# Eight-head decayed scores: two 64-row matmuls per head pair merged into one 128-row matmul against a zero-padded query operand

## The reference

```python
def step(state, xs):                       # one chunk of 64 tokens, all heads
    qc, kc, gc, vc = xs
    cum = jnp.cumsum(gc, axis=2)           # running sum of log f
    diff = cum[:, :, :, None, :] - cum[:, :, None, :, :]
    decay = jnp.exp(jnp.where(causal[:, :, None], diff, -jnp.inf))
    scores = jnp.einsum('bhtk,bhsk,bhtsk->bhts', qc, kc, decay)
    o = (jnp.einsum('bhts,bhsv->bhtv', scores, vc)
         + jnp.einsum('bhtk,bhkv->bhtv', qc * jnp.exp(cum), state))
    ...
```

## Time and profile before

| What | Value |
|---|---|
| Median of 3 runs | 1262.92 us (1262.79 to 1265.36) |
| The profiled execution | 1262.79 us |
| Its span | 1260.8 us |
| PE busy | 1120.0 us (89%) |
| DVE busy | 735.0 us (58%) |
| ACT busy | 613.4 us (49%) |
| POOL busy | 37.3 us (3%) |
| Mean granted TensorE clock | 0.907 |

### The profile page before, as it was taken

The page is one execution under the profiler, slowest core; times in us unless marked ns, Lnnn a source line. Parts: engine busy times, 40 slices in busy tenths (PEclk is TensorE's granted clock), DMA queues, the critical chain, the costliest instruction groups (busy, mean ns, idle before and its releaser), DMA issues.

```text
span 1260.8 us, 14187 instructions
## 1 busy us (share of the span) xinstructions
PE 1120.0 (89%) x5473; PEld 924.3 (73%) x5473; DVE 735.0 (58%) x847; ACT 613.4 (49%) x714; POOL 37.3 (3%) x44
## 2 busy tenths in 40 slices
PE   5999688987499999999986999997899889999997
PEld 4788557966477777777764788886787767788886
DVE  4444224554757787877876556554638554565554
ACT  5444460032267777778774543443446324444341
POOL 0000014300000000000000000000000000000000
PEclk8999965598579999999998999998889769999999
DMA  8766211014158989989884855654322013555520
GB/s 288 253 194 199 67 38 63 18 67 155 35 176 310 343 306 331 325 311 339 313 315 167 300 182 184 196 175 162 110 91 68 1 34 100 169 198 178 188 100 34
DMA packets 116693, 223.30 MB, mean 177 GB/s; under 512 B 6118, under 2 KB 12381, under 8 KB 116638
## 3 DMA queue, kind: packets, MB, share of 16 engines
q1 hardware_dynamic: 112562, 216.76, 50.1%
q10 hardware_dynamic: 3708, 4.57, 1.0%
q0 software_dynamic: 368, 1.21, 0.3%
HBM read 221.45 MB, written 1.07 MB: 176 GB/s over the span
## 4 chain that ended last, share of the span: by engine, by line
PE 72%; DVE 14%; ACT 8%; issue 4%; ACTq 1%; POOL 0%; DMA 0%; DVEq 0%
PE ps L1567 16%; PE ps L1568 15%; PE ps L1569 15%; DVE w_lo L855 7%; PE ps L1817 5%; ACT w_hi L495 4%; PE ps L1818 4%; PE ps L1843 2%; PE ps L2049 2%; PE ps L1863 2%; PE ps L1692 1%; DVE y_lo L1228 1%; ACT y_hi L683 1%; PE ps L2012 1%; PE ps L1557 1%
## 5 line engine op out<-in xcount | busy, mean ns | idle before, releaser
L855 DVE TENSOR_TENSOR w_lo<-w_raw,w_hi 128x2048 fp32r<-128x2048 f32 x204 | 465.4, 2289 | 248.6 <-ACT w_hi L495 248.4
L495 ACT ACTIVATE w_hi<-w_raw 128x2048 fp32r<-128x2048 f32 x204 | 388.5, 1913 | 278.0 <-PE ps L1569 229.4
L1567 PE MATMUL ps<-w_hi,h_hi 128*128 128x512 f32 (+1 forms) x720 | 281.7, 391 | 17.4 <-DVE h_lo L882 7.5
L1568 PE MATMUL ps<-w_lo,h_hi 128*128 128x512 f32 (+1 forms) x720 | 278.2, 386 | 0.0
L1569 PE MATMUL ps<-w_hi,h_lo 128*128 128x512 f32 (+1 forms) x720 | 277.8, 386 | 0.0
L1567 PEld LDWEIGHTS ps<-w_hi,h_hi 128*128 128x128 f32 x720 | 139.0, 193 | 46.1 <-DVE h_lo L882 8.6
L1569 PEld LDWEIGHTS ps<-w_hi,h_lo 128*128 128x128 f32 x720 | 138.3, 192 | 26.9
L1568 PEld LDWEIGHTS ps<-w_lo,h_hi 128*128 128x128 f32 x720 | 139.0, 193 | 26.0
L1567 PE MATMUL ps<-w_hi,aT_hi 128*128 128x512 f32 x176 | 69.5, 395 | 7.8 <-DVE aT_lo L1136 6.0
L1569 PE MATMUL ps<-w_hi,aT_lo 128*128 128x512 f32 x176 | 69.2, 393 | 0.0
L1568 PE MATMUL ps<-w_lo,aT_hi 128*128 128x512 f32 x176 | 69.2, 393 | 0.0
(11 more groups left out here) (330 smaller groups left out, 1411.1 us busy)
## 6 DMA issues: line engine op xcount, KB each, us to landing
w_raw<-in_ffn_w_in SPq DMA_DIRECT2D x44, 1024.0 KB, 5.2
w_raw<-in_w_exp_gate SPq DMA_DIRECT2D x32, 1024.0 KB, 5.2
w_raw<-in_w_exp_up SPq DMA_DIRECT2D x32, 1024.0 KB, 5.9
w_raw<-in_w_exp_down SPq DMA_DIRECT2D x32, 1024.0 KB, 6.9
w_raw<-in_w_in SPq DMA_DIRECT2D x22, 1024.0 KB, 5.8
w_raw<-in_ffn_w_out SPq DMA_DIRECT2D x22, 1024.0 KB, 5.0
w_raw<-in_w_mix_in SPq DMA_DIRECT2D x8, 1024.0 KB, 5.2
w_raw<-in_w_out SPq DMA_DIRECT2D x4, 1024.0 KB, 5.0
```

Of the source, the lines that this page charges most:

```text
L495: act.activation(w_hi[:, u % SPLIT, :], w_raw[:, u % RAW, :], ACT.Copy).then_inc(hi_ready, 1)
L855: dve.tensor_tensor(w_lo[:, u % SPLIT, :], w_raw[:, u % RAW, :], w_hi[:, u % SPLIT, :], ALU.subtract).then_inc(lo_ready, 1)
L1567: pe.matmul(out, hi, w_h, start=first, stop=False)
L1568: pe.matmul(out, hi, w_l, start=False, stop=False)
```

## The change

The two heads of a pair are taken in one matmul. The moving operand becomes [128 rows, 2 x 64 columns]: in its first 64 columns the rows of the odd head are zero, in the other 64 those of the even head. Then the contraction over 128 rows gives each head's scores side by side, in 128 columns of one bank. To make this operand, `q_dec` gets two parts (`par`), and each is made by a `scalar_tensor_tensor` that multiplies also by `half_rows[:, par]`, a column that is 1 in the rows of that head and 0 in the others. `half_rows` was there already.

- DVE: line 991 becomes two instructions of 512 elements; line 1005 likewise.
- PE: line 1692 becomes 8 matmuls a level, 128 rows, 128 moving columns, and PSUM banks go by token tile. `level_done` is raised when each tile's four are done, so the first comes at mid-level.
- DVE: `keep` goes by token tile, and still copies 2 x 512 elements a level.
- PE: line 1705 becomes 4 matmuls, 128 rows, 256 moving columns; line 1009 copies as many elements in another order.
- `q_dec` takes two more 1024-element chunks of `arena` that are free at that time.

```diff
-        q_dec = [chunks_1k[:, 7, :], chunks_1k[:, 8, :]]
+        q_dec = [chunks_1k[:, 7:9, :], chunks_1k[:, 0::15, :]]
...
-                for par in range(2):
-                    dve.wait_ge(level_done, counted(n - 1) + par + 1)
-                    dst = near[:, :, par, :].rearrange("p c (n two h) -> p c n two h", two=2, h=h)[:, :, :, 1, :]
-                    dve.copy_predicated(dst, m, ps[:, 4 * (n % 2) + par, :].rearrange("p (c n h) -> p c n h", c=8, h=h)).then_inc(level_kept, 1)
+                for tt in range(TT):
+                    dve.wait_ge(level_done, counted(n - 1) + tt + 1)
+                    dst = tok[:, tt, :].rearrange("p (c n two h) -> p c n two h", c=8, two=2, h=h)[:, :, :, 1, :]
+                    m = masks[:, n - 1:n, :].broadcast_to([P, 8, P]).rearrange("p c (n two h) -> p c n two h", two=2, h=h)[:, :, :, 1, :]
+                    dve.copy_predicated(dst, m, ps[:, 4 * (n % 2) + tt, :].rearrange("p (c n h) -> p c n h", c=8, h=h)).then_inc(level_kept, 1)
...
-                dve.tensor_tensor(halves(q_dec[b], h)[:, :, 1, :], halves(qh_f, h)[:, :, 1, :], halves(pre_f, h)[:, :, 1, :],
-                                  ALU.mult).then_inc(qdec_ready, 1)
+                for par in range(2):
+                    i = dve.scalar_tensor_tensor(out=halves(q_dec[b][:, par, :], h)[:, :, 1, :], in0=halves(qh_f, h)[:, :, 1, :],
+                                                 scalar=half_rows[:, par:par + 1], in1=halves(pre_f, h)[:, :, 1, :],
+                                                 op0=ALU.mult, op1=ALU.mult)
+                i.then_inc(qdec_ready, 1)
...
-            dve.tensor_copy(sc_far.rearrange("p c e t -> p e c t"), ps[:, 0:2, :].rearrange("p e (c t) -> p e c t", c=4)).then_inc(level_kept, 1)
+            dve.tensor_copy(sc_far.rearrange("p (b c) e t -> p b (c e t)", b=2), ps[:, 0:2, :]).then_inc(level_kept, 1)
...
-                        for par in range(2):
-                            r = slice(par * DH, (par + 1) * DH)
-                            q = q_dec[b][r, c0:c0 + P].rearrange("p (n two h) -> p n two h", two=2, h=h)[:, :, 1, :]
-                            i = pe.matmul(ps[:, 4 * (n % 2) + par, ct * DH + tt * S:ct * DH + tt * S + DH],
-                                          k_dec[r, b, ct, tt * P:(tt + 1) * P], q, start=True, stop=True)
-                            if tt == 1 and ct == 3:
-                                i.then_inc(level_done, 1)
+                        q = q_dec[b][:, :, c0:c0 + P].rearrange("p e (n two h) -> p e n two h", two=2, h=h)[:, :, :, 1, :]
+                        i = pe.matmul(ps[:, 4 * (n % 2) + tt, ct * P:(ct + 1) * P], k_dec[:, b, ct, tt * P:(tt + 1) * P], q,
+                                      start=True, stop=True)
+                    i.then_inc(level_done, 1)
...
-                for par in range(2):
-                    r = slice(par * DH, (par + 1) * DH)
-                    i = pe.matmul(ps[:, par, ct * P:ct * P + P], k_dec[r, 1, ct, 0:P],
-                                  q_dec[1][r, ct * S + P:(ct + 1) * S], start=True, stop=True)
+                i = pe.matmul(ps[:, ct // 2, (ct % 2) * S:(ct % 2 + 1) * S], k_dec[:, 1, ct, 0:P],
+                              q_dec[1][:, :, ct * S + P:(ct + 1) * S], start=True, stop=True)
```

More of the change, by code:

```diff
@@ L979, in keep @@
                 dve.wait_ge(level_kept, counted(n - 1))
-                near = sc_near.rearrange("p t c e q -> p (t c) e q")
-                m = masks[:, n - 1:n, :].broadcast_to([P, 8, P]).rearrange("p c (n two h) -> p c n two h", two=2, h=h)[:, :, :, 1, :]
-                for par in range(2):
-                    dve.wait_ge(level_done, counted(n - 1) + par + 1)
-                    dst = near[:, :, par, :].rearrange("p c (n two h) -> p c n two h", two=2, h=h)[:, :, :, 1, :]
-                    dve.copy_predicated(dst, m, ps[:, 4 * (n % 2) + par, :].rearrange("p (c n h) -> p c n h", c=8, h=h)).then_inc(level_kept, 1)
+                for tt in range(TT):
[3 more added lines that the diff above has]
+                    dve.copy_predicated(dst, m, ps[:, 4 * (n % 2) + tt, :].rearrange("p (c n h) -> p c n h", c=8, h=h)).then_inc(level_kept, 1)
             for level in range(LEVELS):
@@ L1004, in _ @@
             dve.wait_ge(level_done, counted(LEVELS - 1))
-            dve.tensor_tensor(q_dec[1].rearrange("p (c s) -> p c s", s=S)[:, :, P:S], qhT[:, :, P:S], pre[:, :, P:S],
-                              ALU.mult).then_inc(qdec_ready, 1)
+            for par in range(2):
+                i = dve.scalar_tensor_tensor(out=q_dec[1][:, par, :].rearrange("p (c s) -> p c s", s=S)[:, :, P:S], in0=qhT[:, :, P:S],
+                                             scalar=half_rows[:, par:par + 1], in1=pre[:, :, P:S], op0=ALU.mult, op1=ALU.mult)
+            i.then_inc(qdec_ready, 1)
             keep(LEVELS)
             dve.wait_ge(far_ready, 1)
-            dve.tensor_copy(sc_far.rearrange("p c e t -> p e c t"), ps[:, 0:2, :].rearrange("p e (c t) -> p e c t", c=4)).then_inc(level_kept, 1)
+            dve.tensor_copy(sc_far.rearrange("p (b c) e t -> p b (c e t)", b=2), ps[:, 0:2, :]).then_inc(level_kept, 1)
             dve.wait_ge(osq_ready, 1)
```

## The result

The changed kernel takes 1269.1 us (median; its runs lie from 1263.3 to 1278.7 but for two strays of 1456 and 3696) against 1262.79 on the same chip: ratio 1.0055, 95% interval 1.0035 to 1.0075. It is slower by 6 to 7 us. The forecast was 1262.8, no change; the time lies near the top of the range. The profiled execution took 1269.43 us, its span is 1267.4, 6.6 longer than the earlier trace rows.

A forecast was written before the change was run, and what follows sets the result against it. PE, DVE and POOL were taken as nearly level, PE setting the pace. Levels and tail add 7.8 us and the risen clock gives 7.8 back: 1262.8 + 7.8 - 7.8 = 1262.8 us, range 1259.5 to 1269.5.

The forecast's parts named there:

- Turns: In the levels, two-input instructions of DVE and POOL do not stream together; their closed loop takes 3.58 us.
- case A: Steady level: POOL goes between DVE's two `q_dec` parts; 4.15 us, +0.57 on 3.58; chance 0.36 with a risen clock.
- Level 1: Second level of the recurrence, with POOL between the two `q_dec` parts: +1.1 us.
- level 2: Third level of the recurrence: 5.35 us after against 3.75 before, +1.6 us.
- There it buys nothing: Within the level loop, a risen PE clock gains nothing, since DVE and POOL bound it.
- case B: Levels: DVE keeps the turn for both `q_dec` parts; 4.05 to 4.13 us a level; chance 0.16 with a risen clock.
- Net in case A: 0.0: Whole kernel: +7.8 us from levels and tail, -7.8 from the risen clock, so no change.
- no turns: Rival, levels: the scalar form takes no turns with POOL; 3.27 or 3.41 us a level, 1256.5 us; chance 0.09.
- PE's cost: Score matmuls: 16 passes of 0.213 us, 3.41 us a level against 3.62, a gain of 0.2 on PE alone.
- The clock: Rises within the level loop; gives back 1.7 us at far scores, 4.9 at values, 1.2 at branch projections.
- The tail: Behind the levels: 0.67 us for `q_dec`'s second part, 1.45 for the far product, +2.1 at clock 0.50.
- the swings' rival: Clock swings, 0.50 at the far product and rising in or behind it; some 4 us given back, 1266.6; chance 0.19.

The follow-up runs named there:

- PE's part alone: Against the kernel before: merged PE matmuls, one plain unmasked `q_dec` read twice, heads not separated; 1257.62 us against 1262.94, ratio 0.996.
- DVE's part alone: Against the changed kernel: `q_dec` still in two masked parts, PE as before the change; 1273.28 us against 1262.94 for the kernel before, ratio 1.0095.
- case B's form: Changed kernel with queries masked once ahead of the levels and `q_dec` as one tensor_tensor of 1024 elements; 1262.89 us against 1261.82, ratio 1.0002.
- the last run: Changed kernel with a small POOL memset ahead of `suf`, and first-tile value products not waiting for the far scores' copy; 1262.29 us against 1261.61, ratio 0.9992.

## Why the prediction was wrong

- **What bounds the kernel** was right: three engines nearly level, a closed loop of DVE and POOL of 3.58 us. PE's part alone left the levels at 3.55 with PE waiting.
- **Turns** were right: in the steady levels DVE ends 0.55 us behind POOL, and `suf` 0.91 to 1.01 behind DVE. The Trainium skill's "GPSIMD Engine Reference", section "Key points", says that GpSimd shares its SBUF interfaces with VectorE, and that instructions of VectorE with two inputs in SBUF contend with it. The traces agree: line 1000 is stretched before and the parts of `q_dec` after, while the copies, whose data come from PSUM, stay at 1.30 us a pair. That section gives no order and no length, and those are what counted.
- **The step that failed** is the steady level of case A: "first part to 0.79, POOL's 2196 to 1.75, second part to 2.35", with POOL's 2191 behind it. It gave DVE's first part the first turn because `q_dec` had it in the earlier trace rows with the same 0.04 us of head start. With the new form POOL's `suf` went first. It was over early, so `k_dec` stood ready and took the turn between the two parts: two turns lost where one was priced, a pair of 3.33 us instead of 2.31, a level of 5.16 instead of 4.15. Level 1 fails by 0.95 and level 2 by 1.05 in the same way. In sum +11.05 for the levels against 5.7.
- Losing the first turn alone costs next to nothing: where PE at clock 0.50 held `k_dec` back, a level was 4.17 to 4.19 us, in the change once and with DVE's part alone three times. So the clock's rise, which pays behind the levels, cost about 1 us in each of the last two; the prediction had "There it buys nothing".
- With the first turn given back the forecast level is there: 4.03 with a constant scalar, 4.09 with POOL 0.04 us later, 4.1 in case B's form. The whole sum is too: 56.0 us with POOL's small delay against 56.1, the "Net in case A: 0.0". In the sum for level 2 the terms give 5.37 where 5.35 is written, which changes nothing.
- That "no turns" was priced as a rival and "the other engine's turn first" was not is the gap: the choice was seen only for the turn between the two parts.
- **PE's cost** was right: passes start 0.213 us apart at 0.50 and 0.112 at 1.00, where 16 take 2.05. Its own time is nowhere on the path of the levels; it acts only by when `k_dec` may start.
- **The clock** was right in what it gave back, -4.9 for the values and -1.3 for the branch (forecast -1.2), and half right in how: it swung, with PE waiting 2.4 to 3.4 us in five of six levels, and cost the far scores 2.51 us where 1.7 was written. The tail is +1.1 instead of +0.4. The Trainium skill's "TensorE: Matmul & The Clock Gate", section "A second HAM failure mode: psum-queue depth-cycling", has such swings between bursts, and the stretches agree with it (five changes from 214 to 249 us). In the version with ScalarE's masks they fell into the values and ate 3.3 us.
- **`keep`, the far copy and `level_done`** cost nothing, as forecast: pairs of 1.30 and 2.45 us, far copy 1.23.
- **Range and chances.** The time lies inside the stated range by luck, since nothing that the range was made of has a level of 5.16 us. "Slower" came about through neither rival as it was priced. The clock was at 0.50 when the far scores began and rose within them, as the swings' rival says, but it gave back 7.1 of the 7.8 us (0.9 at the far scores, 4.9, 1.3) and not some 4. What made the kernel slower is a loop worse than case A's.
- Open: what in the instruction is late, if anything is (that it is the scalar's fetch is argued, the runs show only that the first turn goes with a scalar in SBUF); and what lets the clock fall within the values in some versions and not in others.

## What to carry to other kernels

Where two engines share a path in whole-instruction turns and start within 0.1 us of each other, ask of each edit who will come first, and count the turns lost, not the instruction's own time. A new operand form can change the order and hardly the duration (0.75 us against 0.69), and a tiny delay or a wait on the other engine can be worth more than a saved instruction. An engine off the critical path still sets when another one may start: PE at the higher clock let `k_dec` in earlier and made the last levels longer. Work taken off PE where another engine closes the loop paid here only through the clock behind it, and a version was faster than the kernel before by 0.4% only with the levels back at 3.57 us and that clock kept.

## What the runs showed of the hardware that was not expected

- A scalar_tensor_tensor with its scalar in SBUF, started 0.04 us ahead of POOL, lost the turn to it (pair 3.33 us, with POOL's next instruction in between as well); with a constant scalar, or with POOL 0.08 us behind, it kept it (2.15 and 2.23).
- With passes at clock 0.50 that held `k_dec` back by 1.0 us the same pair took 2.3 us and the level 4.17 to 4.19, where it took 5.16 with passes at 1.00.
- A busier PE did not mean a higher clock: in the last run the clock was 1.00 from 235 to 245 us with PE busy 6.74 us of 10 in merged matmuls; before, it was 0.50 with PE 99% busy in 64-row ones.
